# Inverse roots of the norms as exp(-ln/2) on ScalarE in place of a square root and VectorE's reciprocal

## The reference

```
inv = rsqrt(mean(x * x, axis=-1) + EPS)     # one value for each token
y   = x * inv * gain
h   = h + 0.5 * gate * ((silu(y @ w_gate) * (y @ w_up)) @ w_down)
```

## Time and profile before

| what | value |
|---|---|
| median of 3 runs | 1639.53 us (1638.13 to 1641.22) |
| the profiled execution, its own time | 1638.08 us |
| span of its trace | 1636.4 us |
| granted TensorE clock, mean | 0.999 |
| DVE busy | 1154.6 us (71%) |
| ACT busy | 799.3 us (49%) |
| POOL busy | 171.4 us (10%) |
| moved from and to memory | 315.62 MB, mean 193 GB/s |

### The profile page before, as it was taken

The page is one execution under the profiler, slowest core; times in us unless marked ns, Lnnn a source line. Parts: engine busy times, 40 slices in busy tenths (PEclk is TensorE's granted clock), DMA queues, the critical chain, the costliest instruction groups (busy, mean ns, idle before and its releaser), DMA issues.

```text
span 1636.4 us, 33817 instructions
## 1 busy us (share of the span) xinstructions
PE 1612.3 (99%) x13617; PEld 1574.8 (96%) x13617; DVE 1154.6 (71%) x1452; ACT 799.3 (49%) x973; POOL 171.4 (10%) x193
## 2 busy tenths in 40 slices
PE   6999999999999999999999999999999999999999
PEld 4999999999999999999999999999999999999999
DVE  6877789778766657666688876656665588776653
ACT  3444445355544455444564654445444465564442
POOL 1100114500000000000052200000000035200000
PEclk9999999999999999999999999999999999999999
DMA  9998897645766477755744566568665764456653
GB/s 333 310 315 247 248 331 227 218 153 183 183 190 186 132 195 203 196 164 160 232 139 130 147 178 190 150 180 222 192 184 146 206 189 130 129 158 191 176 160 114
DMA packets 501553, 315.62 MB, mean 193 GB/s; under 512 B 14815, under 2 KB 489674, under 8 KB 501450
## 3 DMA queue, kind: packets, MB, share of 16 engines
q1 hardware_dynamic: 491824, 282.33, 60.6%
q0 software_dynamic: 8496, 29.92, 5.3%
q10 hardware_dynamic: 1130, 1.90, 0.3%
HBM read 313.04 MB, written 1.05 MB: 192 GB/s over the span
## 4 chain that ended last, share of the span: by engine, by line
PE 71%; DVE 4%; ACT 2%; issue 1%; ACTq 0%; DVEq 0%
PE accs L1750 20%; PE accs L1752 20%; PE accs L1751 19%; PE wide L1790 1%; PE accs L1790 1%; PE accs L1788 1%; PE wide L1788 1%; PE accs L1789 1%; PE wide L1789 1%; DVE wlo L1063 1%; PE wide L2021 1%; PE accs L1848 1%; PE accs L1850 0%; PE accs L1849 0%; PE ps_score L2070 0%
## 5 line engine op out<-in xcount | busy, mean ns | idle before, releaser
L1750 PE MATMUL accs<-uhi_shift,whi 128*128 128x256 f32 x2304 | 650.9, 283 | 3.0 <-DVE ulo L1114 1.2
L1752 PE MATMUL accs<-uhi_shift,wlo 128*128 128x256 f32 x2304 | 645.4, 280 | 0.0
L1751 PE MATMUL accs<-ulo,whi 128*128 128x256 f32 x2304 | 643.2, 279 | 0.0
L749 ACT CAST whi<-raw 128x2048 fp32r<-128x2048 f32 (+2 forms) x294 | 499.7, 1702 | 106.4 <-PE accs L1752 58.7
L1063 DVE TENSOR_TENSOR wlo<-raw,whi 128x2048 fp32r<-128x2048 f32 (+2 forms) x249 | 496.4, 2001 | 4.5 <-ACT gat L990 3.1
L1750 PEld LDWEIGHTS accs<-uhi_shift,whi 128*128 128x128 f32 x2304 | 433.6, 188 | 11.4 <-issue 5.2
L1751 PEld LDWEIGHTS accs<-ulo,whi 128*128 128x128 f32 x2304 | 434.1, 188 | 1.2 <-issue 1.2
L1752 PEld LDWEIGHTS accs<-uhi_shift,wlo 128*128 128x128 f32 x2304 | 433.4, 188 | 0.0
L1750 PE MATMUL accs<-hhi_room,whi 128*128 128x256 f32 x1056 | 296.0, 280 | 0.8 <-DVE wlo L1063 0.8
L1752 PE MATMUL accs<-hhi_room,wlo 128*128 128x256 f32 x1056 | 294.7, 279 | 0.0
L1751 PE MATMUL accs<-hlo_room,whi 128*128 128x256 f32 x1056 | 294.6, 279 | 0.0
(11 more groups left out here) (368 smaller groups left out, 2261.0 us busy)
## 6 DMA issues: line engine op xcount, KB each, us to landing
raw<-in_ffn_w_in SPq DMA_DIRECT2D x176, 512.0 KB, 5.1
in_turn<-in_w_ada POOLq DMA_DIRECT2D x56, 512.0 KB, 5.7
raw<-in_w_mix_in SPq DMA_DIRECT2D x52, 512.0 KB, 4.7
raw<-in_ffn_w_out SPq DMA_DIRECT2D x64, 384.0 KB, 3.6
raw<-in_w_ff_gate SPq DMA_DIRECT2D x44, 512.0 KB, 5.0
raw<-in_w_ff_up SPq DMA_DIRECT2D x44, 512.0 KB, 6.5
raw<-in_w_in SPq DMA_DIRECT2D x40, 512.0 KB, 5.2
raw<-in_ffn_w_out SPq DMA_DIRECT2D x64, 320.0 KB, 4.0
```

The lines of the kernel that those rows point to most:

```text
L749: nc.scalar.copy(whi[:, n % RING, 0:cols], raw[:, n % RING, 0:cols]).then_inc(hi_ready, 1)
L1750: mm(dst, wh, xh, start=first, stop=False)
L1751: mm(dst, wh, xl, start=False, stop=False)
L1752: return mm(dst, wl, xh, start=False, stop=last)
```

## The change

Each inverse root is made by ScalarE alone, as exp(-0.5 * ln(mean + eps)): Ln in place of Sqrt, then Exp in place, with the signal to VectorE behind Exp. VectorE's five lines of code with reciprocals (ten instructions, since three norms run through one of them and five through another) are gone; the waits ahead of them stay. In the double norm both pairs stand one behind the other on ScalarE.

```diff
@@ root_of_mean
-                nc.scalar.activation(rstd[:, 0:w], ps_stat[:, 0:w], ACT.Sqrt, bias=eps[:], scale=1.0 / D).then_inc(rms, 1)
+                link(nc.scalar.activation(rstd[:, 0:w], ps_stat[:, 0:w], ACT.Ln, bias=eps[:], scale=1.0 / D))
+                nc.scalar.activation(rstd[:, 0:w], rstd[:, 0:w], ACT.Exp, scale=-0.5).then_inc(rms, 1)
@@ final_norms (ScalarE)
-                nc.scalar.activation(rstd[:, 0:T], sumsq_f[:, 0], ACT.Sqrt, scale=1.0 / D).then_inc(rms_f, 1)
-                nc.scalar.activation(rstd_f, ps_stat[:, 0:T], ACT.Sqrt, bias=eps[:], scale=1.0 / D).then_inc(rms_f, 1)
+                link(nc.scalar.activation(rstd[:, 0:T], sumsq_f[:, 0], ACT.Ln, scale=1.0 / D))
+                nc.scalar.activation(rstd[:, 0:T], rstd[:, 0:T], ACT.Exp, scale=-0.5).then_inc(rms_f, 1)
+                link(nc.scalar.activation(rstd_f, ps_stat[:, 0:T], ACT.Ln, bias=eps[:], scale=1.0 / D))
+                nc.scalar.activation(rstd_f, rstd_f, ACT.Exp, scale=-0.5).then_inc(rms_f, 1)
@@ root
                 dve.wait_ge(rms, STATS.index(name) + 1)
-                link(nc.vector.reciprocal(rstd[:, 0:T], rstd[:, 0:T]))
@@ scale_of
                 dve.wait_ge(rms, STATS.index(name) + 1)
-                link(nc.vector.reciprocal(rstd[:], rstd[:]))
@@ final_residual
                 dve.wait_ge(rms_f, 2)
-                link(nc.vector.reciprocal(rstd_f, rstd_f))
```

## The result

The changed kernel takes 1646.48 us in the median of 15 runs (1642.13 to 1650.71), the kernel before, beside it, 1639.53 us in the median of 15 (1636.92 to 1644.82). The ratio is 1.0043, 95% interval 1.0034 to 1.0053: **slower by 0.43%, about 7 us**. I had forecast 4 us more (1643.5) and a range that ended at 1646.5, where the measured median lies. The profiled execution took 1645.97 us, 7.9 more than that of before.

A forecast was written before the change was run, and what follows sets the result against it. TensorE's work was taken to bound the kernel; 4.0 us from the double norm and 0 from the other eight, added to the 1639.5 us median, gave 1643.5 us, with a range of 1640.0 to 1646.5 us.

The forecast's parts named there:

- What bounds the kernel: TensorE, busy 1612.3 of 1636.4 us; removing VectorE's reciprocals could win only a 0.6 us wait at the double norm.
- Two tables for Ln and Exp: At each norm, Ln and Exp use different tables, so a 1283 ns load precedes each; four loads at the double norm.
- third rival: Ln and Exp share a table, so the double norm's first silu starts as now: 1639.5 us, not slower.
- The single norms at nothing: At the eight other norms, later ScalarE work such as a silu 0.5 us late is covered: 0 us in total.
- The double norm: Ahead of ffn(2), queued loads start the first silu 4.0 us late, and TensorE's fourth chunk waits the whole 4.0 us.
- the clock: TensorE's clock behind the double norm's wait: nothing added in the sum; at half clock, 1.65 us more in a rival.
- second rival: The wait at ffn(2)'s fourth chunk also lowers TensorE's clock, losing 1.65 us more: 1645.2 us; chance 0.30.
- the chance of slower: Whole kernel slower by over 0.2%, over 1642.8 us: four fifths of the first case, all second and fifth; 0.73.
- the fifth case: A later chunk or the mixers' preloads cost as well, 3 us or more on top (1647 us); chance 0.07.

The follow-up runs named there:

- order by function: Changed kernel with the double norm's operations ordered Ln, Ln, Exp, Exp, two table loads fewer: 1638.2 us against 1638.42 for the kernel before, ratio 1.0000.
- loads alone: Kernel before plus three table loads (Ln, Exp, Ln) behind the double norm's second square root, nothing computed from them: 1641.14 us against 1638.42, ratio 1.0017.
- four matmuls: Changed kernel plus four unread constant matmuls ahead of ffn(2)'s fourth chunk, where TensorE waits: 1643.38 us against 1638.42 for the kernel before, ratio 1.0023.

## Why the prediction was wrong

- **What bounds the kernel**, right: 17.0 us less on VectorE gained nothing. The kernel with the order by function has all ten reciprocals gone as well and takes the time of before, 1.0000 [0.9991, 1.0009].
- **Two tables for Ln and Exp**, right: a load at both lines of each norm, four at the double one. The third rival, one table for both (0.07), was no case here: the trace has both loads in every norm. A load is measured at 1283 ns, and at the double norm the next instruction starts within 0.02 us behind it, so nothing beside those 1.28 us had to be priced.
- **The single norms at nothing**, right, 0.9992 [0.9982, 1.0003]. The silu is 0.5 us late and covered. The preload in in1 and in2 is still carried out (1.28 us on ScalarE, twice), and TensorE does not wait for it.
- **The double norm**, right in place, order and size: 4.0 us late at the silu, 3.91 us at the fourth chunk, the bank wait unchanged at 0.6, and 3.9 us between the runs with the clock's part taken out. The kernel with the loads alone shows that loads in the queue ahead of the silu are enough for such a wait, and the order by function shows that this queue is what matters, not the number of roots.
- **The step that failed is the clock, put at 0 in the sum and priced only in the second rival: "At half the clock 3.3 us of wall time do 1.65 us of work, so 1.65 us more are lost: 1645.2 us. I give it 0.30."** The price of one stretch was right. But I counted one stretch, once, and as the lesser chance. The runs show some 2.1 stretches more than before, and none of 21 runs without any, where 26 of 56 of before had none: 2.1 x 1.7 = 3.6 us. With the wait that is 7.5 us, and 7 were measured (part of a stretch can lie in the wait itself, where it is free). The mis-sized term is 3.6 in place of 0 in the sum, or of 1.65 in its rival. Filling the wait with four matmuls took most of this term away and left the 4 us.
- The weak point of that step was its evidence. The 3.3 us in that sum are the earlier trace rows, where in in0 the clock was at 0.50 for 3.3 us, behind a 1.6 us wait: one fall, and I took its length for that of every fall, and a wait of 4 us for one of the same order. (The same wait, of 1.66 us, stands in the trace of the order by function, and the clock stays at 1.00 there; so even that fall is not explained by the wait alone.) I also took dense work around the wait for a protection; behind the 3.9 us here the clock was at 0.50 for 6.8 us all the same.
- **Small misses.** ScalarE gained 17.9 us where 14 to 17 were expected; ten Exp and ten loads make 17.0, and the rest is open. By its own terms the chance of slower is 0.38 + 0.30 + 0.07 = 0.75, not 0.73.
- **The range** ended on the measured median (1646.48 against 1646.5; by the ratio it is 1646.6), and 7 of the 15 runs lie above it. It was too narrow on that side: it priced the clock at one stretch at most, and what lay above only through other waits (the fifth case), which did not come.

## What to carry to other kernels

When a matmul-bound kernel gets a new wait of a few us in dense work, price the wait and TensorE's clock behind it, and let the range reach to twice the wait (here 7 us for 4, with the clock at 0.50 for 3.41 or 6.8 us in the traces behind the 3.9 us wait, and at 1.00 behind one of 2.8); the mean granted clock of each run tells the two apart, and the trace tells where the clock fell. In an engine's queue count what stands ahead of a result that is wanted now and is itself wanted later (here a pair not yet wanted, which made the silu 4.0 us late): group the activations by function, and place both the second root and the wait for it just ahead of their use. Work moved off an engine where TensorE wasn't waiting for it gave nothing here: all ten reciprocals are gone from VectorE in the order by function, at a ratio of 1.0000.

## What the runs showed that I had not expected

- After a wait of 3.9 us in otherwise full work the granted clock was at 0.50 for 3.41 or 6.8 us in the two traces; after one of 2.8 us at the same place the runs had no more such stretches than before. What happens between was not tried.
- The same program has 0 to 2 such stretches, which differ from one execution to the next (before: clock 1.000 in 26 of 56 runs, 1637.3 and 1637.0 us in the two batches; 0.998 in 22, 1641.0 and 1639.8). Much of the spread of this kernel's times goes with this.
- The preload of Exp in in1 and in2, with Exp's table already in, still took 1.28 us on ScalarE each time (L918).
- A 128x512 fp32 matmul, not in the fp32r form of the weights, was carried out as two instructions and took 0.8 to 0.9 us (7.3 us for nine, x18 in the timeline; four of them 3.6, x8).
